# Modulation products on the unsplit fp32 slab, in four column quarters of the array and in runs of four

## The reference

```python
def _adaln(cvec, w, b):
    m = (jax.nn.silu(cvec) @ w + b)[:, None, :]
    return jnp.split(m, 6, axis=-1)

for l in range(DEPTH):
    mod_p = _adaln(c_ctx[None, :], w_mod[l], b_mod[l])     # w_mod[l]: 2048 x 12288
    mod_s = _adaln(c, w_mod[l], b_mod[l])
    hp = _modulate(xp, norm1_g[l], mod_p[0], mod_p[1])     # rms norm * (1 + scale) + shift
    ... attention or recurrence, output projection ...
    xp = xp + mod_p[2] * out_p
    hp = _modulate(xp, norm2_g[l], mod_p[3], mod_p[4])
    xp = xp + mod_p[5] * _conv_ffn(hp, ...)
```

## Time and profile before

| | |
|---|---|
| median of three runs | 3097.68 us (3096.56 to 3100.39) |
| profiled execution | 3094.88 us |
| its span, first to last instruction | 3093.1 us |
| PE busy | 2834.5 us, 92% of the span |
| VectorE busy | 2061.7 us, 67% |
| ScalarE busy | 1616.4 us, 52% |
| moved from HBM | 601 MB, 196 GB/s over the span |

### The profile page before, as it was taken

How to read it: one execution, slowest core, us unless ns; L and a number is a source line. 1 busy time by engine, 2 the same in 40 slices (tenths; PEclk the granted TensorE clock), 3 DMA queues, 4 the chain that set the end, 5 groups by cost and what they waited for, 6 DMA issues and landing times. The chain is left out here.

```text
span 3093.1 us, 43144 instructions
## 1 busy us (share of the span) xinstructions
PE 2834.5 (92%) x15008; PEld 2235.7 (72%) x15008; DVE 2061.7 (67%) x2334; ACT 1616.4 (52%) x1903; POOL 0.5 (0%) x6
## 2 busy tenths in 40 slices
PE   6799966979999999999997999857879999999997
PEld 2477746757777777778885778545668888888885
DVE  7866645777777777777667774154466666667676
ACT  6555522546666666665554663212335555555553
POOL 0000000000000000000000000000000000000000
PEclk9899976989999999999998999667789999999998
DMA  9688810766888888885544885011245555555462
GB/s 379 258 273 267 274 43 1 247 215 224 274 267 276 265 275 266 274 268 193 185 161 167 271 275 156 21 45 55 103 143 171 184 185 187 185 188 185 166 208 84
DMA packets 171523, 607.91 MB, mean 197 GB/s; under 512 B 18680, under 2 KB 26872, under 8 KB 171128
## 3 DMA queue, kind: packets, MB, share of 16 engines
q1 hardware_dynamic: 170872, 603.12, 58.1%
q10 hardware_dynamic: 512, 2.97, 0.2%
HBM read 601.38 MB, written 4.63 MB: 196 GB/s over the span
## 5 line engine op out<-in xcount | busy, mean ns | idle before, releaser
L421 DVE TENSOR_TENSOR w_lo<-raw,w_hi 128x1024 fp32r<-128x1024 f32 x1140 | 1370.7, 1223 | 750.2 <-ACT w_hi L414 745.7
L414 ACT ACTIVATE w_hi<-raw 128x1024 fp32r<-128x1024 f32 x1140 | 1170.7, 1054 | 935.8 <-PE banks L542 863.2
L541 PE MATMUL banks<-xs_ffn,w_hi 128*128 128x512 f32 x4224 | 1505.6, 400 | 15.5 <-DVE xs_ffn L674 14.7
L542 PE MATMUL banks<-xs_ffn,w_lo 128*128 128x256 f32 x4224 | 1188.7, 281 | 0.0
L541 PEld LDWEIGHTS banks<-xs_ffn,w_hi 128*128 128x128 f32 x4224 | 797.3, 189 | 227.6 <-issue 16.3
L542 PEld LDWEIGHTS banks<-xs_ffn,w_lo 128*128 128x128 f32 x4224 | 802.1, 190 | 5.6
L501 PE MATMUL banks<-w_hi,cond_split 128*4 128x512 f32 x768 | 304.9, 397 | 37.2 <-PEq L562 22.0
L501 PE MATMUL banks<-w_lo,cond_split 128*4 128x512 f32 x768 | 303.3, 395 | 0.0
L541 PE MATMUL banks<-xs_even,w_hi 128*128 128x512 f32 x576 | 209.2, 404 | 7.1 <-DVE xs_even L674 7.1
L541 PE MATMUL banks<-xs_odd,w_hi 128*128 128x512 f32 x512 | 185.6, 403 | 7.5 <-DVE xs_odd L674 7.1
L541 PE MATMUL banks<-xs_out,w_hi 128*128 128x512 f32 x512 | 184.5, 402 | 8.2 <-DVE xs_out L704 8.2
(11 more groups left out here) (282 smaller groups left out, 1988.0 us busy)
## 6 DMA issues: line engine op xcount, KB each, us to landing
raw<-in_w_mod SPq DMA_DIRECT2D x384, 512.0 KB, 4.7
raw<-in_ffn_w_up SPq DMA_DIRECT2D x352, 512.0 KB, 3.6
raw<-in_ffn_w_down SPq DMA_DIRECT2D x176, 512.0 KB, 3.3
raw<-in_even_w_in SPq DMA_DIRECT2D x72, 512.0 KB, 4.4
raw<-in_odd_w_in SPq DMA_DIRECT2D x64, 512.0 KB, 4.5
raw<-in_even_w_out SPq DMA_DIRECT2D x32, 512.0 KB, 4.4
raw<-in_odd_w_out SPq DMA_DIRECT2D x32, 512.0 KB, 3.3
raw<-in_odd_w_tail SPq DMA_DIRECT2D x8, 448.0 KB, 3.6
```

The costliest lines, as they stand in the source:

```text
L414: act.activation(w_hi[:, s % SPLIT], raw[:, s % RAW], ACT.Copy).then_inc(hi_done.sem, 1)
L421: dve.tensor_tensor(w_lo[:, s % SPLIT], raw[:, s % RAW], w_hi[:, s % SPLIT].bitcast(F32), ALU.subtract).then_inc(lo_done.sem, 1)
L541: pe.matmul(bank, w_hi[:, slot, c, cols], moving[:, c, :], start=start and c == 0, stop=False)
L542: mm = pe.matmul(bank[:, 0:NT], w_lo[:, slot, c, cols], moving[:, c, 0:NT], start=False, stop=stop and c == CHUNKS - 1)
```

## The change

A mod slab is no longer split. PE multiplies it as it lies in `raw`, in plain fp32, by the unsplit conditioning vectors `cond`, which are padded with zeros from 2 to 32 columns. The 16 chunks of a group go in turn to four quarters of the array's columns, so the partial sums stand in four quarters of the bank's rows; `copy_mod_rows` copies all 128 rows and `turn_mod` adds the four quarters by its constant. Own and mod slabs go in runs of four instead of one by one. The slot of a mod slab comes free when PE has used it (`mod_used`) and that of an own slab when it has been split; the splits count own slabs alone and run four own slabs ahead; in the first phase there are no splits but those of the next phase's first four own slabs.

```diff
+BATCH = 4
+QUAD = 32
+QUADS = P // QUAD
@@ constants
-        c[stream, C_SUM + stream] = 1.0
-        c[2 + stream, C_SUM + stream] = 1.0
+        c[stream::QUAD, C_SUM + stream] = 1.0
@@ Phase
             if own and mod:
-                self.seq += [own[0], *(slab for pair in zip(own[1:], mod) for slab in pair), mod[-1]]
+                for k in range(0, per_group, BATCH):
+                    self.seq += own[k:k + BATCH] + mod[k:k + BATCH]
@@ trunk
-        cond_split = sb("cond_split", [P, KD, 4], F32R)
-        mod_rows = sb("mod_rows", [4, 2, SLABW])
+        cond = sb("cond", [P, KD, QUAD])
+        mod_rows = sb("mod_rows", [P, 2, SLABW])
@@ load_slab
-            wait(sp, hi_done.sem, in_slot_before)
-            wait(sp, lo_done.sem, in_slot_before)
+            what, count = in_slot_before
+            if what == "own":
+                wait(sp, hi_done.sem, count)
+                wait(sp, lo_done.sem, count)
+            else:
+                wait(sp, mod_used.sem, count)
@@ split_stream
-                for s in range(f.slabs):
+                for s, (kind, g, k) in enumerate(f.seq):
                     run_pieces(f, places, i, s, first, left)
-                    ahead = s + SPLIT
+                    if kind == "mod":
+                        continue
+                    ahead = f.own_at.index(s) + SPLIT
...
+            if not owns:
+                for o in range(SPLIT):
+                    split(eng, f.next, 0, o)
@@ product_stream
-                    pe.wait_ge(lo_done.sem, f.slab(i, s) + 1)
                     if kind == "mod":
-                        products = mod_products(pe, f, i, s, g, k)
+                        pe.wait_ge(*slab_landed(f, i, s))
+                        mod_products(pe, f, i, s, g, k).then_inc(mod_used.sem, 1)
                     else:
+                        o = f.own_at.index(s)
+                        pe.wait_ge(lo_done.sem, f.own(i, o) + 1)
@@ mod_products
             for c in range(CHUNKS):
-                for n, half in enumerate((w_hi, w_lo)):
-                    mm = pe.matmul(banks[0:4, MOD_ROWS + j % 2, :], cond_split[:, CHUNKS * k + c, :],
-                                   half[:, s % SPLIT, c, :], start=(k == 0 and c == 0 and n == 0),
-                                   stop=(k == MOD_SLABS - 1 and c == CHUNKS - 1 and n == 1))
+                n = CHUNKS * k + c
+                quad = QUAD * (n % QUADS)
+                mm = pe.matmul(banks[quad:quad + QUAD, MOD_ROWS + j % 2, :], cond[:, n, :], raw[:, s % RAW, c, :],
+                               start=n < QUADS, stop=n >= KD - QUADS)
@@ copy_mod_rows
-            act.activation(mod_rows[:, j % 2, :], banks[0:4, MOD_ROWS + j % 2, :], ACT.Copy).then_inc(rows_out.sem, 1)
+            act.activation(mod_rows[:, j % 2, :], banks[:, MOD_ROWS + j % 2, :], ACT.Copy).then_inc(rows_out.sem, 1)
@@ turn_mod
-                               const[0:4, C_SUM:C_SUM + 2], start=True, stop=True)
+                               const[:, C_SUM:C_SUM + 2], start=True, stop=True)
@@ first block
-                    act.wait_ge(act_step.sem, 1)
-                    act.activation(cond_split[:, :, 0:2], cond_f[:], ACT.Copy).then_inc(act_step.sem, 1)
-                    for s in range(SPLIT):
-                        split_hi(act, first, 0, s)
...
-                    for s in range(SPLIT):
-                        split_lo(dve, first, 0, s)
+                    dve.memset(cond[:], 0.0).then_inc(dve_step.sem, 1)
```

More of the change, by code:

```diff
@@ L197, in __init__ @@
         self.slabs = len(self.seq)
+        self.own_at = [s for s, slab in enumerate(self.seq) if slab[0] == "own"]
+        self.mod_at = [s for s, slab in enumerate(self.seq) if slab[0] == "mod"]
         self.ends = [self.seq.index(("own", g, per_group - 1)) for g in range(groups)]
@@ L200, in __init__, with own, mod_slab, used @@
         self.by_halves = by_halves
-        self.slab0 = self.group0 = self.mod0 = self.half0 = 0
+        self.own0 = self.group0 = self.mod0 = self.half0 = 0
         self.slot0 = [0] * RAW
-        self.before = [0] * RAW
+        self.before = [("own", 0)] * RAW
         self.next = None
         self.continues = False
-    def slab(self, i, s):
-        return self.slab0 + i * self.slabs + s
+    def own(self, i, o):
+        return self.own0 + i * len(self.own_at) + o
+    def mod_slab(self, i, m):
+        return (self.mod0 + i * self.mods) * MOD_SLABS + m
+    def used(self, i, s):
+        if self.seq[s][0] == "own":
+            return "own", self.own(i, self.own_at.index(s)) + 1
+        return "mod", self.mod_slab(i, self.mod_at.index(s)) + 1
     def group(self, i, g):
@@ L227, in plan @@
 def plan(phases):
-    slab = group = mod = half = 0
-    held, last = [0] * RAW, [0] * RAW
+    own = group = mod = half = 0
+    held, last = [0] * RAW, [("own", 0)] * RAW
     for n, ph in enumerate(phases):
-        ph.slab0, ph.group0, ph.mod0, ph.half0 = slab, group, mod, half
+        ph.own0, ph.group0, ph.mod0, ph.half0 = own, group, mod, half
         ph.slot0, ph.before = list(held), list(last)
@@ L237, in plan @@
             if k:
-                last[slot] = slab + (ph.iters - 1) * ph.slabs + slot + RAW * (k - 1) + 1
-        slab += ph.iters * ph.slabs
+                last[slot] = ph.used(ph.iters - 1, slot + RAW * (k - 1))
+        own += ph.iters * len(ph.own_at)
         group += ph.iters * ph.groups
@@ L395, in body @@
                 for s in range(RAW, f.slabs):
-                    load_slab(sp, f, i, s, f.slab(i, s - RAW) + 1)
+                    load_slab(sp, f, i, s, f.used(i, s - RAW))
                 if last:
@@ L401, in body @@
                         newest = s + RAW * (f.loads_of(s) - 1)
-                        load_slab(sp, f, i + 1, s, f.slab(i, newest) + 1)
+                        load_slab(sp, f, i + 1, s, f.used(i, newest))
             rolled(sp, f.iters, body)
@@ L407, in slab_landed, with split_hi, split_lo @@
             return landed[slot].sem, 16 * (f.slot0[slot] + i * f.loads_of(slot) + s // RAW + 1)
-        def split_hi(act, f, i, s):
-            q = f.slab(i, s)
+        def split_hi(act, f, i, o):
+            q, s = f.own(i, o), f.own_at[o]
             act.wait_ge(*slab_landed(f, i, s))
             wait(act, slab_used.sem, q - SPLIT + 1)
-            act.activation(w_hi[:, s % SPLIT], raw[:, s % RAW], ACT.Copy).then_inc(hi_done.sem, 1)
-        def split_lo(dve, f, i, s):
-            q = f.slab(i, s)
+            act.activation(w_hi[:, o % SPLIT], raw[:, s % RAW], ACT.Copy).then_inc(hi_done.sem, 1)
+        def split_lo(dve, f, i, o):
+            q, s = f.own(i, o), f.own_at[o]
             dve.wait_ge(hi_done.sem, q + 1)
             wait(dve, slab_used.sem, q - SPLIT + 1)
-            dve.tensor_tensor(w_lo[:, s % SPLIT], raw[:, s % RAW], w_hi[:, s % SPLIT].bitcast(F32),
+            dve.tensor_tensor(w_lo[:, o % SPLIT], raw[:, s % RAW], w_hi[:, o % SPLIT].bitcast(F32),
                               ALU.subtract).then_inc(lo_done.sem, 1)
         def split_stream(eng, f, split, places, also=None, left=()):
+            owns = len(f.own_at)
             def body(i, first, last):
-                for s in range(f.slabs):
+                for s, (kind, g, k) in enumerate(f.seq):
                     run_pieces(f, places, i, s, first, left)
-                    ahead = s + SPLIT
-                    if ahead < f.slabs:
+                    if kind == "mod":
+                        continue
+                    ahead = f.own_at.index(s) + SPLIT
+                    if ahead < owns:
                         due = f, i, ahead
                     elif not last:
-                        due = f, i + 1, ahead - f.slabs
+                        due = f, i + 1, ahead - owns
                     else:
-                        due = f.next, 0, ahead - f.slabs
+                        due = f.next, 0, ahead - owns
                     if due[0] is not None:
@@ L484, in body @@
                         if f.by_halves:
-                            products = slab_products(i, s, g, k, out if k == 0 else 0)
+                            products = slab_products(i, o, g, k, out if k == 0 else 0)
                         else:
-                            products = slab_products(i, s, g, k)
-                    products.then_inc(slab_used.sem, 1)
+                            products = slab_products(i, o, g, k)
+                        products.then_inc(slab_used.sem, 1)
                     run_pieces(f, places, i, s, first, left)
@@ L507, in copy_mod_rows @@
             n = f.mod_group(i, j)
-            act.wait_ge(slab_used.sem, f.slab(i, f.mod_ends[j]) + 1)
+            act.wait_ge(mod_used.sem, f.mod_slab(i, MOD_SLABS * j + MOD_SLABS - 1) + 1)
             wait(act, rows_turned.sem, n - 1)
-            act.activation(mod_rows[:, j % 2, :], banks[0:4, MOD_ROWS + j % 2, :], ACT.Copy).then_inc(rows_out.sem, 1)
```

(10 more changed lines are left out.)

21 lines of the change are left out of this document (10 added, 11 removed).

## The result

The changed kernel takes 2971.52 us (median of four runs, 2969.39 to 2987.95) against 3097.12 for the kernel before, run beside it: ratio 0.9605, 95% interval 0.9569 to 0.9641. Six more runs have the median 2982.85 us, ratio 0.9658 (0.9632 to 0.9684).

A forecast was written before the change was run, and what follows sets the result against it. PE was taken to bound the mixed stages, DMA the first. From 3094.9 us, 131 for the batches and 15 for stage starts came off, giving 2949; 2.8 added made 2952 as a median, range 2910 to 3090.

The forecast's parts named there:

- Four at a time: Modulation products on PE: four quarters run at once, 2.01 us a batch against 3.65, 80 batches, -131 us; 60% chance.
- The entry: Entering and leaving the column quarters on PE costs 0.29 us a batch, with 0 and 0.6 as bounds.
- Strict order: Rival on PE: no instruction starts before the one ahead of it; a batch takes 4.16 us, 3124 us in all; 7%.
- 13 us less: Gain on PE's batches reduced if quarters reach only the skill's 2.38 for three tiles: about 2.2 us instead of 1.72.
- Starts: First groups of three mixed stages: modulation slabs need no split, saving 5 of 8 us each, -15 us (0 to 24).
- The turn: Turn of a finished group and its copy: 128 rows instead of 4, columns set the time; 0 to -8 us.
- The first stage: Stage of modulation slabs only stays bound by DMA, 10.4 us a group against PE's 8.0: zero (0 to -5).
- Bank emptying between the groups: Between a group's last own slab and the next group's first, a 2.0 us batch replaces 1.8 us of cover: no cost.
- The paragraph on the loads: Mixed stages: loads go out in one burst per eight slabs; own slabs land in time, 1.0 us to spare.
- DMA hidden: Mixed stages: eight slabs load in 12.8 us against PE's 13.8, so transfers stay hidden, near 305 GB/s.

The follow-up runs named there:

- one quarter: Against the changed kernel, all modulation products go to one quarter of the array's columns, with order, splits and loads unchanged: 3401.02 us.
- Runs of two: Against the changed kernel, the next own slabs' loads are issued before the modulation loads, and BATCH = 2: 3002.93 us, ratio 0.9706 to the kernel before.
- Own loads first: Against the changed kernel, SyncE issues the next four own loads ahead of the four modulation loads: 2949.61 us, ratio 0.9546 to the kernel before.
- splits three ahead: Against the changed kernel, ScalarE and VectorE split own slabs three ahead instead of four, loads unchanged: 2954.45 us, ratio 0.9557 to the kernel before.

## Why the prediction was right, and where it was off

Faster, 2971.5 or 2982.9 us for 2952 forecast, inside the range. By the terms of its sum:

- *Four at a time, 2.01 us a batch in place of 3.65*: right. Four own slabs and a batch take 13.35 us (11.49 and 1.86), of which 32 pairs of own products at 0.354 make 11.33, so a batch costs 2.02. Before, by the same count, (31.03 - 64 x 0.354 - 1.08) / 2 = 3.65. 80 batches gain 130 us; forecast 131. The entry, priced at 0.29 from the switch between 128 and 16 rows, measures 0.14 in the batch and 0.16 in the own run.
- *Strict order*, a rival, fell: a quarter's second instruction does not hold back the next quarter. In the batch with one quarter the wait for the second slab's landing stands at the fifth weight load, with four at the third, though the products stand in the program in the same order; so with four, the first instructions of four matmuls (306.913 to .933) start before the second of any (from 307.367). The Trainium skill, "TensorE: Matmul & The Clock Gate", section "Part 3: Packing small matmuls — row/col tiling", says that matmuls start and end strictly in program order. For whole matmuls the batch agrees, as the second instructions start in the same order as the first ones, 307.367 to .387; for the two instructions of each it does not. In the earlier trace rows whole matmuls disagree as well: the upper half's first instruction starts at 453.99 and the last three of the lower half's sixteen at 454.09 to 454.31. The same section's 2.38 for three column tiles is 79% of three; the runs show 6.98 / 1.86 = 3.8 for four, 94%. The prediction's "13 us less" by that figure set 2.2, without the entry, against 2.01, with it; with the entry in both it would have been 36.
- *Starts, -15*: right. The first groups behind a norm lost 6.9, 6.4 and 6.9 us against a steady 31.03. Now, less their wait at the end (0.9, 2.1 and 0.6), they lose 1.7, 1.8 and 1.8 against 27.56. That is 14.9.
- *The turn, 0 with -8 as its bound*: it went to the bound. 1.08 became 0.86, 9 us in 40 groups. *The first stage, 0*: -2.5.
- *Bank emptying between the groups, "Nothing"*: the step that failed, +46 us. The cover named for it was not the thing that counted. Runs of two show that 1.0 us would do; the copy and the add came late, since late splits stood ahead of them. The paragraph on the loads held the cause: it found the burst, the four own loads behind four that wait for PE, and asked only whether an own slab lands in time for its own product, which it does. It didn't ask what stands behind the splits in the programs of ScalarE and VectorE. Own loads first and splits three ahead each take most of the 46 away.
- *DMA hidden*: right as a matter of bandwidth, 305 GB/s in the mixed stage as forecast.

Together -130 - 9 - 15 - 2.5 + 46 = -110.5; the last stage's pace adds -13.9 and that of ten own groups without modulation (22.61 to 22.19 us each) -4, so -128.4 where the span shows -125.5. The other 3 us are small differences elsewhere, among them 1.6 more in the second `out` stage, which ran at the slower pace after the change. The pace had no place in the forecast; that it made up for 18 of the 46 us in this profile is luck. Without the waits at the group ends the change would have come near its forecast: own loads first spans 2944.8 with the last stage at 750.0 us, as in the first profile of before, so 148 less than 3093.1, of which 4 are the pace of those ten groups; -146 was forecast. The two come so close because the 14 us of waits that are left there stand against the 9 of the turn and the 2.5 of the first stage, which were forecast at nothing.

The better version is the changed kernel with own loads first. It is shown only that the remaining 14 us of waits sit at 9 group ends, not what makes these late.

## What to carry to other kernels

When an edit makes transfers come in bursts, follow the late slab past its own use: what else stands behind the operation that waits for it, on that engine, and who needs that. Narrow matmuls side by side in the array's columns pay only if enough of them stand in a run to fill all parts, because each entry and exit costs as well (0.3 us here, a third of a former slab). And two cures for one wait need not add up: loading earlier and splitting later pull at the same slots.

## What the runs showed that was not expected

- Four column quarters work at 94% of four times one (1.86 us against 6.98 / 4 = 1.75), in fp32. The two instructions of one matmul don't follow each other there: those of the other quarters start in between.
- The same stage of the same kernel takes 736.1 or 750.0 us, 4224 products at 0.347 or 0.354 us a pair over hundreds of microseconds, at granted clock 1.00 in both. What decides it was not found. At 13.9 us it is more than a third of what own loads first gained, so such kernels are better compared stage by stage.
